# Four tiles' gate products ahead of their additions, in place of tile by tile, on one core

## The reference

```python
xn = rms_norm(x, norm_mix[l])
h = xn @ w_in[l]                       # q, k, v of three attentions, and hg, the gates
... # o_a, o_b, o_c: three attention branches, each (512, 512)
branches = jnp.stack([o_a, o_b, o_c], axis=2)
proj = jnp.einsum('bsgc,gcd->bsgd', branches, w_branch[l])
gates = jax.nn.sigmoid(hg.reshape(b, s_len, N_BRANCHES, d))
x = x + jnp.sum(gates * proj, axis=2) @ w_out[l]
```

## Time and profile before

| what | value |
|---|---|
| time, median of 3 runs | 1525.47 us (1524.52 to 1525.71) |
| the profiled execution | 1524.72 us, its span 1522.6 us |
| PE busy | 1468.6 us, 96% of the span |
| DVE busy | 925.8 us, 61% |
| ACT busy | 860.9 us, 57% |
| POOL busy | 397.5 us, 26% |
| chain that ended last | PE 83%, DVE 8%, ACT 3%, issue 2%, DMA 2% |
| mean granted clock of TensorE | 0.988 |

### The profile page before, as it was taken

One profiled execution on the slowest core, in us unless ns is written; L12 is line 12 of the kernel. 1 busy time (PEld: TensorE's weight loads), 2 busy tenths in 40 slices (PEclk: granted clock), 3 DMA queues, 4 the chain that ended last, 5 costly groups with the idle time before them and its releaser, 6 DMA issues.

```text
span 1522.6 us, 22440 instructions
## 1 busy us (share of the span) xinstructions
PE 1468.6 (96%) x7894; PEld 1142.2 (75%) x7894; DVE 925.8 (61%) x1806; ACT 860.9 (57%) x1660; POOL 397.5 (26%) x554
## 2 busy tenths in 40 slices
PE   8999999999999999999899999999999999999994
PEld 6887777677777787777678867776677777877773
DVE  3555655544554447999854566645445544489996
ACT  5446656655453335888644655565554433468883
POOL 3414227520000013453105053195000000225211
PEclk9999999999999999999999999999999999999997
DMA  7722222142232357999876321222422323769996
GB/s 187 137 76 64 63 60 68 55 117 60 67 97 84 115 185 240 351 364 349 292 192 115 80 63 53 67 70 56 106 67 63 111 84 105 246 224 370 370 360 238
DMA packets 155384, 231.06 MB, mean 152 GB/s; under 512 B 20579, under 2 KB 89955, under 8 KB 155268
## 3 DMA queue, kind: packets, MB, share of 16 engines
q1 hardware_dynamic: 143780, 209.62, 45.6%
q0 software_dynamic: 10768, 17.80, 3.5%
q10 hardware_dynamic: 720, 2.16, 0.4%
HBM read 220.99 MB, written 29.69 MB: 165 GB/s over the span
## 4 chain that ended last, share of the span: by engine, by line
PE 83%; DVE 8%; ACT 3%; issue 2%; DMA 2%; ACTq 0%; SPq 0%; POOLq 0%; DVEq 0%
PE bank L545 22%; PE bank L547 20%; PE bank L546 20%; PE bank L1673 4%; PE bank L1658 3%; PE bank L1649 3%; PE bank L1651 3%; DVE xT L617 2%; PE bank L648 2%; ACT xT L611 2%; DVE gate_t L2094 1%; PE bank L1705 1%; DMA q_c<-ytok 1%; PE bank L1708 1%; PE bank L1644 1%
## 5 line engine op out<-in xcount | busy, mean ns | idle before, releaser
L545 PE MATMUL bank<-wh,xT 128*128 128x512 f32 (+1 forms) x960 | 399.3, 416 | 6.5 <-DVE gate_t L2094 4.7
L547 PE MATMUL bank<-wh,xT 128*128 128x512 f32 (+1 forms) x960 | 374.1, 390 | 0.0
L546 PE MATMUL bank<-wl,xT 128*128 128x512 f32 (+1 forms) x960 | 373.3, 389 | 0.0
L486 ACT ACTIVATE wh<-raw,gcol 128x512 fp32r<-128x512 f32 (+1 forms) x208 | 149.0, 717 | 204.6 <-PE bank L547 204.6
L493 DVE SCALAR_TENSOR_TENSOR wl<-raw,gcol,wh 128x512 fp32r<-128x512 f32 (+1 forms) x208 | 161.4, 777 | 135.5 <-ACT wh L486 128.5
L545 PEld LDWEIGHTS bank<-wh,xT 128*128 128x128 f32 x960 | 180.8, 188 | 73.3 <-issue 23.0
L547 PEld LDWEIGHTS bank<-wh,xT 128*128 128x128 f32 x960 | 180.4, 188 | 37.5
L546 PEld LDWEIGHTS bank<-wl,xT 128*128 128x128 f32 x960 | 181.3, 189 | 29.8 <-issue 1.4
L2032 DVE CUSTOM_DVE_ANT_0 prob<-bank,mask 128x128 f32<-128x128 f32 (+3 forms) x128 | 60.5, 490 | 190.0 <-PE bank L1649 100.9
L1820 ACT ACTIVATE prob<-prob,nmax 128x128 f32<-128x128 f32 (+3 forms) x192 | 107.4, 561 | 113.2 <-DVE nmax L2032 112.9
L2336 POOL TENSOR_TENSOR rows<-x_rows,ac 128x512 f32<-128x512 f32 x16 | 22.2, 1404 | 502.8 <-DVE x_rows L2103 502.8
(11 more groups left out here) (334 smaller groups left out, 2711.9 us busy)
## 6 DMA issues: line engine op xcount, KB each, us to landing
raw<-in_w_in_dram SPq DMA_DIRECT2D x192, 256.0 KB, 2.7
bqkv<-in_w_expert_gate_dram SPq DMA_DIRECT2D x64, 256.0 KB, 5.6
bqkv<-in_w_expert_up_dram SPq DMA_DIRECT2D x64, 256.0 KB, 7.8
bqkv<-in_w_expert_down_dram SPq DMA_DIRECT2D x32, 512.0 KB, 8.5
q_c<-in_w_expert_gate_dram SPq DMA_DIRECT2D x64, 256.0 KB, 5.8
q_c<-in_w_expert_up_dram SPq DMA_DIRECT2D x64, 256.0 KB, 8.2
head_odd<-in_w_expert_down_dram SPq DMA_DIRECT2D x32, 512.0 KB, 8.8
raw<-in_w_branch_dram SPq DMA_DIRECT2D x48, 256.0 KB, 2.6
```

The lines of the kernel that those rows point to most:

```text
L486: nc.scalar.activation(wh[:, i % HL, 0:width], raw[:, i % RAW, 0:width], ACT.Copy, scale=piece_gain(i))\
L545: nc.tensor.matmul(out, lhs[0], rhs[0], start=start, stop=False)
L546: nc.tensor.matmul(out, lhs[0], rhs[1], start=False, stop=False)
L547: return nc.tensor.matmul(out, lhs[1], rhs[0], start=False, stop=stop)
```

## The change

For branches 2 to 5 the addition to rows leaves the read of a tile. At the ends of branches 2, 3 and 4 it moves into after_read, where each tile's addition is followed at once by the wait for it and by the count for ACT. At OUT0 the four additions follow the four reads, without waits between them. The number and shapes of the instructions that compute are the same.

```diff
                     else:
-                        m = 4 * (idx - 2) + n
                         nc.vector.scalar_tensor_tensor(out=gate_t[:, n, :], in0=gate_t[:, n, :], scalar=1.0,
                                                        in1=src, op0=ALU.add, op1=ALU.mult).then_inc(acc_read, 1)
-                        sums_read(dve, g, n)
-                        nc.vector.tensor_tensor(rows[:, n, cs], rows[:, n, cs], gate_t[:, n, :], ALU.add)\
-                            .then_inc(merged, 1)
...
+            def merge(idx, n):
+                cs = slice(512 * (idx % 2), 512 * (idx % 2 + 1))
+                nc.vector.tensor_tensor(rows[:, n, cs], rows[:, n, cs], gate_t[:, n, :], ALU.add).then_inc(merged, 1)
+
             def after_read(g, n):
 
                 name, idx, _, _ = GROUPS[g]
                 if name not in ("qk", "uq", "ukv", "v", "small", "branch"):
                     return
+                sums_read(dve, g, n)
                 if name == "branch" and idx >= 2:
+                    merge(idx, n)
                     dve.wait_ge(merged, of(merged, 4 * (idx - 2) + n + 1))
-                sums_read(dve, g, n)
                 s_ = {"v": v_copied, "small": small_copied, "branch": branch_ready}.get(name, rows_copied)
                 dve.sem_inc(s_, 1)
...
                     if s == OUT0:
                         for n in range(NT):
                             read_group(PIECES[s - 1][0], n)
+                        for n in range(NT):
+                            sums_read(dve, PIECES[s - 1][0], n)
+                            merge(GROUPS[PIECES[s - 1][0]][1], n)
                         dve.wait_ge(merged, of(merged, 16))
```

## The result

The changed kernel took 1527.94 us (median of 12 runs, 1523.20 to 1529.01), the kernel before beside it 1524.42 us (1521.84 to 1526.46). The ratio is 1.0025, with a 95% interval of 1.0018 to 1.0033: 3.8 us slower (2.7 to 5.0). The profiled execution took 1528.47 us, its span is 1526.4 us, against 1524.72 and 1522.6.

The account below looks back on a forecast made before the run. TensorE, busy 96% of the span, was taken as the bound. + 1.8 us without the clock and + 3.3 us for clock falls gave + 5.1 us: 1529.8 us for the profiled execution, range 1525.4 to 1534.8 us.

Parts of the forecast that it names:

- The stalls on the banks: Behind branches 2 to 5, TensorE's waits for the gate product (14 times, 4.7 us in all) would go.
- Behind branch 5 the term: At OUT0, TensorE's first piece would take 2.72 us in place of 4.33: gain 1.61 us a layer.
- Behind branch 4: No attention pairs: the bank stall goes, TensorE waits 0.44 us for a later low part; gain 1.32 us a layer.
- Layer 1 repeats them: The steps behind the branch groups in layer 0 were taken to recur in layer 1, 752.00 us later.
- The lost cover: Behind branches 2 and 3, additions leave DVE's wait for scores; scaling and TensorE's turn come 1.91 and 1.90 us later.
- the wait between two additions: On DVE, each addition's own wait and count for ACT was taken as 0.23 us: 0.69 + 0.23 = 0.92 us an addition.
- the sum without the clock: Per layer + 1.91 + 1.90 - 1.32 - 1.61 = + 0.88 us; two layers + 1.8 us.
- The clock: Four TensorE idle times of 2.5 us, even odds of a clock fall each: two falls at 1.65 us, + 3.3 us.
- That the clock hardly falls: Rival: low part as forecast, clock holds behind the idle times; + 1.8 us, 1527.3 us; chance 0.15.
- a round trip longer than 0.23 us: Rival: at 0.35 us an addition takes 1.04 us, three or four clock falls; about 1535 to 1537 us; chance 0.10.
- That an own wait costs little: Rival: additions on DVE come every 0.69 us and the clock should hold; - 2.8 us, 1522.7 us; chance 0.09.
- That the stalls are gained and nothing is given back: Rival: slack of the probabilities' turn absorbs the later scaling; - 9.0 us, 1516.5 us; chance 0.04.

Follow-up runs that it names:

- Run 5: Changed kernel, but additions of tiles 0 and 1 behind branch 2 and 3 right behind their products: 1518.74 us, ratio 0.9963 to the kernel before.
- run 6: Changed kernel, but the four additions behind branch 2, 3 and 4 back to back, then the four waits and counts: 1520.93 us, ratio 0.9985 to the kernel before.
- run 1: Changed kernel plus 14 identity transposes on TensorE before the probabilities' turn behind branch 2 and 3: 1524.77 us, ratio 1.0001 to the kernel before.
- run 7: Changed kernel, but tiles 0 and 1 of branch 2 and 3 added in the cover, other additions behind scaling or low part: 1515.37 us, ratio 0.9936.
- run 3: Changed kernel, but branch 4 and 5 tile by tile, products first only behind branch 2 and 3: 1530.70 us, ratio 1.0046 to the kernel before.
- runs 1 and 4: The second: products first behind branch 2 and 3 alone, plus 14 identity transposes before the probabilities' turn there: 1531.26 us, ratio 1.0044 to the kernel before.

## Why the prediction was right, point by point

**The stalls on the banks** all go, as forecast. Behind branch 5 the term was 1.61 us and measured 1.61. Behind branch 4 it was 1.32 us and measured 1.60 in layer 1 and 1.25 in layer 0. That 1.25 is so near is luck: the additions came sooner than forecast, and a gap of 0.58 us in front of the low part, taken as 0.23, made up for it. The kernel before already had 0.61 us there in layer 0; the prediction read that gap in layer 1 alone, so that its "Layer 1 repeats them" does not hold for it.

**The lost cover** is the step that carries the sign, and it held: the additions of tiles 0 and 1 leave DVE's wait for scores, the scaling comes later by as much, and TensorE's turn behind it. Run 5 puts the two additions back into the cover, with which their own waits go too, and the loss behind branch 2 and 3 is gone; run 6 gives 0.7 of the 1.63 us to the waits and 0.9 to the cover. The delay was put at 1.91 and 1.90 us and measured 1.63 and 1.63.

**The term that was mis-sized** is the wait between two additions: 0.23 us forecast, an addition every 0.92 us. The additions came every 0.83 us ((3.19 - 0.69) / 3), 0.14 us of idle time between them. What a wait with its count adds is 0.23 us over the 0.60 us at which additions without one follow each other (run 6), and the prediction put 0.23 us on top of the full 0.69 us that an addition takes. The gap of 0.23 us that it went by stands in front of a low part, ahead of which there is one wait more in the program. This made the sum without the clock + 0.4 us (layer 0: 1.63 + 1.63 - 1.25 - 1.61 = + 0.40; layer 1: + 0.05, so + 0.45), where + 1.8 was forecast.

**The clock** was put at two falls of four, + 3.3 us. The profiled execution had three, of up to 1.7 us each (half of 3.42 us at half the clock), and lacked one that the execution before had elsewhere: 0.45 + 3 x 1.7 - 1.65 = + 3.9 us, against 1528.47 - 1524.72 = + 3.75. With the 1.5 to 1.6 us a fall that the last section reads from the rows, it is + 3.4. Over all executions, the filler of run 1 puts the falls' part at about 3 us and what is left at 0.7 us by the medians. Most of the measured loss is thus the clock's, as the forecast had it, through a somewhat smaller idle time and, in the traced execution, three falls in place of two. The even odds came from one lull in each layer; that they led so near is in part luck. By the medians the measured + 3.5 us (+ 3.8 by the ratio) lies under the forecast + 5.1 mostly by the wait between additions. In the profiled execution that term (1.35 us too much) and the falls (some 4.6 us for three, where 3.3 was forecast) nearly cancel, and most of what is left is the fall that was missing elsewhere (1.65 us), which the prediction did not have.

**The rivals.** That the clock hardly falls (+ 1.8 us) is refuted by the falls in the traced execution and by run 1, and a round trip longer than 0.23 us by additions 0.83 us apart and not 1.04. That an own wait costs little had 0.09, and reality lies between it (additions 0.69 us apart) and the forecast (0.92). Beside it the prediction weighed a rule of the Trainium skill ("VectorE: DVE Perf Modes", section "The DRAIN you can't avoid"), that a semaphore after each operation costs nothing extra. No run leaves that semaphore out, so none tests the rule by itself: each addition raises one in the changed kernel and in run 6, and in run 6 they follow each other every 0.60 us all the same. What costs time here is more than the rule speaks of, DVE's wait for that semaphore and the count behind it: 3.19 us for four in place of 2.49, 0.23 us for each of three. That the stalls are gained and nothing is given back would have been - 9.0 us; run 7, which makes that world by putting the additions where nobody waits, measured - 9.8 (7.8 to 11.7).

**Left open** is why the gap in front of the low part behind branch 4 is 0.58 us in layer 0 and 0.23 us in layer 1; the kernel before has it as well (0.61 and 0.26 us), so the change did not bring it, but no run was made for its cause. By the mean clocks, the clock fell in nearly every execution of the changed kernel and in two of six of run 3, which has the same idle times; why is not settled either, and only one execution of each was traced. The distances between the idle times differ in the two, but no run separates that.

## What to carry to other kernels

When an instruction is moved out of a loop, look at what the engine was waiting for at the place it leaves: work that stood in front of a wait for another engine was free there, and behind it it cost its full length and the waits between. A stall that goes on the busiest engine is only a gain if the next thing which that engine waits for was not already late; read the wait after the one you remove. And take out of a step what nobody behind it needs, and put it behind what somebody needs (here the additions behind the scaling), with one wait at the end rather than one behind each.

## What the runs showed of the hardware

Behind idle times of TensorE of 2.1 to 2.3 us between dense matmuls the granted clock fell from 1.00 to 0.50 at three of four places, in the profiled execution of the changed kernel and in that of run 3, and it stayed there for 3.42 us, although the engine was busy again. One of these falls came only 1.3 us behind the end of the idle time. With the filler it stayed at 1.00 at all eight places of runs 1 and 4, and behind idle times of 1.4 to 1.6 us at the four of run 6, again in one execution of each. The price can be read from the turn behind branch 2 to the next shift on DVE, first in run 3, with a fall:

```profile
398.83 1.12 PE L1658 MATMUL bank<-ident,prob 128*128 128x128 f32 x4 [2.09 <-DVE prob L2042]
...
403.88 0.56 DVE L2032 CUSTOM_DVE_ANT_0 prob<-bank,mask 128x384 f32<-128x384 f32 x1 [4.19 <-PE bank L1651]
```

and in run 6, without one, from 398.27 to:

```profile
401.83 0.56 DVE L2032 CUSTOM_DVE_ANT_0 prob<-bank,mask 128x384 f32<-128x384 f32 x1 [2.69 <-PE bank L1651]
```

That is 5.05 us against 3.56 us, 1.49 us for a fall. The changed kernel shows the same within one execution, behind branch 3, in layer 0 without a fall (from the turn at 454.36) and in layer 1 with one:

```profile
458.96 0.69 DVE L2032 CUSTOM_DVE_ANT_0 prob<-bank,mask 128x512 f32<-128x512 f32 x1 [3.61 <-PE bank L1651]
...
1207.38 1.73 PE L1658 MATMUL bank<-ident,prob 128*128 128x128 f32 x8 [2.31 <-DVE prob L2042]
...
1213.57 0.69 DVE L2032 CUSTOM_DVE_ANT_0 prob<-bank,mask 128x512 f32<-128x512 f32 x1 [5.19 <-PE bank L1651]
```

That is 4.60 us against 6.19 us, 1.59 us for a fall. Fourteen transposes of no use in each of the four idle times made the kernel faster by about 3 us.
